# Expert tokens of a mixture-of-experts decoder step: rows fetched by an indirect DMA instead of one-hot matmuls

## The reference, cut to what matters

```
def moe_swiglu(x, g, w_router, w_eg, w_eu, w_ed):
    h = rms_norm(x, g)
    hf = h.reshape(-1, D_MODEL)
    logits = (hf @ w_router).astype(jnp.float32)
    top_v, top_i = lax.top_k(logits, TOP_K)
    gates = jax.nn.softmax(top_v, axis=-1)
    combine = jnp.einsum('tk,tke->te', gates, jax.nn.one_hot(top_i, N_EXPERTS, ...))
    y = jnp.zeros_like(hf)
    for e in range(N_EXPERTS):
        he = jax.nn.silu(hf @ w_eg[e]) * (hf @ w_eu[e])
        y = y + combine[:, e:e + 1] * (he @ w_ed[e])
    return x + y.reshape(x.shape)
```

## Time and profile before

| | |
|---|---|
| median of 3 runs | 1717.1 us (1715.7 to 1719.49) |
| span of the profiled execution | 1712.6 us |
| TensorE matmul busy | 1595.5 us (93%) |
| VectorE busy | 1169.5 us (68%) |
| ScalarE busy | 954.3 us (56%) |
| GpSimd busy | 673.6 us (39%) |
| DMA | 426.00 MB, mean 249 GB/s |
| mean granted TensorE clock | 0.963 |
| share of the chain of waits that ended last | TensorE 75%, VectorE 13% |

### The profile page before, as it was taken

How to read it: one execution, slowest core, us unless ns; L and a number is a source line. 1 busy time by engine, 2 the same in 40 slices (tenths; PEclk the granted TensorE clock), 3 DMA queues, 4 the chain that set the end, 5 groups by cost and what they waited for, 6 DMA issues and landing times.

```text
span 1712.6 us, 22726 instructions
## 1 busy us (share of the span) xinstructions
PE 1595.5 (93%) x8152; PEld 1334.1 (78%) x8152; DVE 1169.5 (68%) x1150; ACT 954.3 (56%) x991; POOL 673.6 (39%) x235
## 2 busy tenths in 40 slices
PE   6786899999978889999999999999999999999998
PEld 5774899999956868878877877877877887887786
DVE  5998545446784447767767776776786776777775
ACT  5411543344553426756756657666666665766664
POOL 5561111012210025545436445444544544553553
PEclk9888999999987879999999999999999999999999
DMA  8821244444450139969978987987996996996993
GB/s 317 153 94 54 74 148 176 154 142 170 144 210 1 50 139 338 352 246 364 355 266 342 356 328 277 351 333 279 346 349 273 355 351 247 359 358 241 366 348 146
DMA packets 62801, 426.00 MB, mean 249 GB/s; under 512 B 7653, under 2 KB 9957, under 8 KB 12192
## 3 DMA queue, kind: packets, MB, share of 16 engines
q1 hardware_dynamic: 57312, 412.38, 64.4%
q0 software_dynamic: 2432, 8.08, 2.5%
q10 hardware_dynamic: 3008, 4.88, 0.9%
HBM read 418.36 MB, written 7.95 MB: 249 GB/s over the span
## 4 chain that ended last, share of the span: by engine, by line
PE 75%; DVE 13%; issue 7%; ACT 4%; POOL 1%; DMA 0%; ACTq 0%; DVEq 0%
PE bank L326 21%; PE bank L328 21%; PE bank L327 20%; PE bank L662 4%; DVE odd L1142 2%; ACT w_hi L995 2%; DVE C L1142 2%; PE bank L686 2%; DVE w_lo L1087 2%; PE bank L703 2%; DVE pick L1414 1%; PE bank L348 1%; PE bank L582 1%; DVE C L1155 1%; DVE w_lo L1363 0%
## 5 line engine op out<-in xcount | busy, mean ns | idle before, releaser
L1580 POOL TENSOR_TENSOR d_lo<-land,d_hi 128x2048 fp32r<-128x2048 f32 x112 | 538.8, 4814 | 664.9 <-ACT d_hi L998 664.9
L1363 DVE TENSOR_TENSOR w_lo<-land,w_hi 128x2048 fp32r<-128x2048 f32 x224 | 611.9, 2767 | 157.9 <-ACT w_hi L995 157.0
L995 ACT CAST w_hi<-land 128x2048 fp32r<-128x2048 f32 x224 | 417.6, 1912 | 0.0
L326 PE MATMUL bank<-w_hi,xe_hi 128*128 128x512 f32 x896 | 376.0, 420 | 0.5 <-DVE w_lo L1363 0.5
L328 PE MATMUL bank<-w_hi,xe_lo 128*128 128x512 f32 x896 | 353.0, 394 | 0.0
L327 PE MATMUL bank<-w_lo,xe_hi 128*128 128x512 f32 x896 | 350.5, 391 | 0.0
L998 ACT CAST d_hi<-land 128x2048 fp32r<-128x2048 f32 x112 | 214.2, 1914 | 128.9 <-PE bank L328 128.9
L326 PEld LDWEIGHTS bank<-w_hi,xe_hi 128*128 128x128 f32 x896 | 168.8, 188 | 39.7 <-DVE w_lo L1363 7.5
L328 PEld LDWEIGHTS bank<-w_hi,xe_lo 128*128 128x128 f32 x896 | 168.5, 188 | 38.0
L327 PEld LDWEIGHTS bank<-w_lo,xe_hi 128*128 128x128 f32 x896 | 169.3, 189 | 33.2
L326 PE MATMUL bank<-d_hi,heT_hi 128*128 128x512 f32 x448 | 176.8, 395 | 19.7 <-DVE heT_lo L1458 19.7
(11 more groups left out here) (227 smaller groups left out, 2355.9 us busy)
## 6 DMA issues: line engine op xcount, KB each, us to landing
land<-in_w_expert SPq DMA_DIRECT2D x336, 1024.0 KB, 6.7
land<-in_w_dense SPq DMA_DIRECT2D x54, 1024.0 KB, 4.8
rel_rows<-rb POOLq DMA_DIRECT2D x1, 3072.0 KB, 38.0
bias<-rel_rows ACTq DMA_DIRECT2D x4, 512.0 KB, 4.8
X<-in_x SPq DMA_DIRECT2D x4, 288.0 KB, 5.8
out_y<-X SPq DMA_DIRECT2D x2, 576.0 KB, 2.8
Us<-in_state POOLq DMA_DIRECT2D x1, 1088.0 KB, 9.4
out_conv_s<-Us POOLq DMA_DIRECT2D x1, 1088.0 KB, 6.7
```

The lines of the kernel that those rows point to most:

```text
L326: pe.matmul(out, w[0], x[0], start=start, stop=False)
L995: act.copy(w_hi[n % RING][:], land[(DENSE + u) % LAND][:]).then_inc(hi_done, 1)
L1363: dve.tensor_tensor(w_lo[n % RING][:], land[slot][:], w_hi[n % RING][:].bitcast(F32), ALU.subtract).then_inc(split, 1)
L1580: pool.tensor_tensor(d_lo[ch % 2][:], land[slot][:], d_hi[ch % 2][:].bitcast(F32), ALU.subtract).then_inc(d_split, 1)
```

## The change

`H_tok` is now scaled by the inverse norm when it is made (half 0 by GpSimd, half 1 by ScalarE) and stored once to a DRAM tensor `h_rows` of 289 rows, the last of them zero. `PG` is gone, and `pick` holds ones only. A small matmul (slot_rows: `pick` x `tok`, 2 columns, three token tiles) gives for each of the expert's 128 slots the row of its token and its gate. VectorE turns the first into an integer `slot_row`, and GpSimd starts an indirect DMA that fetches 128 rows of 4 KB (0.5 MB) from `h_rows` to `xt`, one row to a partition. gather is then eight plain transposes of `xt`. The gate is applied per slot when `oe` is taken from PSUM, and `oe` is kept in two fp32r parts: ScalarE writes both halves of oe_hi, VectorE both halves of oe_lo. back becomes two fp32r matmuls by `PT`, which now holds ones. The split of the down weights stays on GpSimd.

```diff
-            def gather(h):
+            def gather(trip, h):
+                pe.wait_ge(xt_ready, 16 * (trip + 1))
                 for k in range(4):
-                    for j, (t0, nt) in enumerate(TT):
-                        last = pe.matmul(bank[4 + h][:, P * k:P * k + P],
-                                         H_tok[0:nt, j, (4 * h + k) * P:(4 * h + k + 1) * P],
-                                         pick[0:nt, j, :], start=(j == 0), stop=(j == 2))
+                    last = pe.transpose(bank[4 + h][:, P * k:P * k + P], xt[:, (4 * h + k) * P:(4 * h + k + 1) * P], ident)
+            def slot_rows(out):
+                for j, (t0, nt) in enumerate(TT):
+                    last = pe.matmul(out[:, 0:2], pick[0:nt, j, :], tok[0:nt, j, :], start=(j == 0), stop=(j == 2))
+                last.then_inc(rows_placed, 1)
...
+            pe.wait_ge(P_ready, 1)
+            slot_rows(bank[0])
             pe.wait_ge(htok_ready, 6)
...
-                pe.matmul(out[:, 0:T], oe[:, P * k:P * k + P], PT[:, :], start=True, stop=True).then_inc(y_done, 1)
+                pe.matmul(out[:, 0:T], oe_hi[:, P * k:P * k + P], PT[:, :], start=True, stop=False)
+                pe.matmul(out[:, 0:T], oe_lo[:, P * k:P * k + P], PT[:, :], start=False, stop=True).then_inc(y_done, 1)
...
+                    if ch == GATES_AT + 1:
+                        with pe.If(trip < n_trips - 1):
+                            pe.wait_ge(P_ready, trip + 2)
+                            pe.wait_ge(PT_ready, trip + 2)
+                            slot_rows(bank[7])
...
+            act.wait_ge(htok_scaled, 3)
+            act.wait_ge(htok_ready, 6)
+            for i, (t0, nt) in enumerate(TT):
+                act.dma_start(h_rows[t0:t0 + nt, :], H_tok[0:nt, i, :]).then_inc(h_stored, 16)
...
-                act.copy(oe[:, 0:512], bank[2][:, :]).then_inc(oe_ready, 1)
+                act.wait_ge(gates_ready, trip + 1)
+                for h in range(2):
+                    act.activation(oe_hi[:, 512 * h:512 * h + 512], bank[2 + h][:, :], ACT.Identity,
+                                   scale=slot_gate[:, 0:1]).then_inc(oe_hi_ready, 1)
...
+            def slot_row_of(n, src):
+                dve.wait_ge(rows_placed, n)
+                dve.tensor_scalar(slot_row[:], src[:, 0:1], -1.0, float(T), ALU.mult, ALU.add).then_inc(rows_ready, 1)
...
+                    if ch == GATES_AT + 2:
+                        with dve.If(trip < n_trips - 1):
+                            slot_row_of(trip + 2, bank[7])
-                dve.tensor_copy(oe[:, 512:1024], bank[3][:, :]).then_inc(oe_ready, 1)
+                for h in range(2):
+                    dve.wait_ge(oe_hi_ready, trip * 2 + h + 1)
+                    dve.scalar_tensor_tensor(out=oe_lo[:, 512 * h:512 * h + 512], in0=bank[2 + h][:, :],
+                                             scalar=slot_gate[:, 0:1], in1=oe_hi[:, 512 * h:512 * h + 512].bitcast(F32),
+                                             op0=ALU.mult, op1=ALU.subtract).then_inc(oe_ready, 1)
+                with dve.If(trip < n_trips - 1):
+                    dve.wait_ge(oe_ready, trip * 2 + 4)
+                    dve.tensor_copy(slot_gate[:], bank[7][:, 1:2]).then_inc(gates_ready, 1)
...
+            def gather_rows(trip):
+                pool.wait_ge(rows_ready, trip + 1)
+                pool.indirect_dma_start(xt[:], None, h_rows[:, :],
+                                        bass.IndirectOffsetOnAxis(ap=slot_row[:, 0:1], axis=0)).then_inc(xt_ready, 16)
...
+            pool.wait_ge(h_stored, 48)
+            gather_rows(0)
             expert_lo(0, 0)
             expert_lo(0, 1)
...
                 with pool.If(trip < n_trips - 1):
+                    gather_rows(trip + 1)
                     expert_lo(trip, NCH)
                     expert_lo(trip, NCH + 1)
```

More of the change, by code:

```diff
@@ L172, in build @@
                ("d_lo0", [P, UNIT], F32R), ("d_lo1", [P, UNIT], F32R),
-               ("H_tok", [P, 3, D], F32), ("pick", [P, 3, SLOTS], F32), ("PG", [P, 3, SLOTS], F32),
-               ("PT", [SLOTS, T], F32), ("slot_of", [P, 3, PASSES * NE + 1], F32),
+               ("oe_hi", [SLOTS, D], F32R), ("oe_lo", [SLOTS, D], F32R), ("pick", [P, 3, SLOTS], F32),
+               ("PT", [SLOTS, T], F32R), ("tok", [P, 3, 2], F32), ("slot_row", [SLOTS, 1], I32),
+               ("slot_gate", [SLOTS, 1], F32), ("slot_of", [P, 3, PASSES * NE + 1], F32),
                ("gate_of", [P, 3, PASSES * NE + 1], F32), ("lg", [P, 6, 3, NE], F32), ("rt", [P, 3], F32),
                ("cmp", [P, 2, 3, NE, NE], F32), ("top", [P, 16], F32), ("trips", [1, 2], I32)]
[L177 to L182, removed]
+        (d_hi0, d_hi1, d_lo0, d_lo1, oe_hi, oe_lo, pick, PT, tok, slot_row, slot_gate, slot_of, gate_of, lg, rt,
+         cmp_, top, trips, xe_hi, xe_lo, xt, silu_g, he, heT_hi, heT_lo) = phase(
+            *moe, ("xe_hi", [P, D], F32R), ("xe_lo", [P, D], F32R), ("xt", [SLOTS, D], F32),
+            ("silu_g", [P, CH], F32), ("he", [SLOTS, CH], F32), ("heT_hi", [P, CH], F32R), ("heT_lo", [P, CH], F32R))
+        Hm, H_tok, zero_row = phase(*moe, ("Hm", [P, KT_D, T], F32), ("H_tok", [P, 3, D], F32),
+                                    ("zero_row", [1, D], F32))[-3:]
         d_hi, d_lo = [d_hi0, d_hi1], [d_lo0, d_lo1]
@@ L610, in route_sums @@
                 if k == KT_D - 1:
-                    pe.matmul(STAT[:, 0:32], ident, PT[:, 0:32], start=False, stop=True).then_inc(lg_done, 1)
+                    pe.matmul(STAT[:, 0:32], ident, pick[:, 0, 0:32], start=False, stop=True).then_inc(lg_done, 1)
             def to_tokens(k):
@@ L1366, in _ @@
             dve.wait_ge(kv_stored, 80)
-            dve.memset(oe[:], 0.0).then_inc(oe_ready, 2)
-            dve.memset(PT[:], 0.0).then_inc(PT_ready, 1)
+            dve.memset(oe_hi[:].bitcast(F32), 0.0).then_inc(oe_ready, 1)
+            dve.memset(oe_lo[:].bitcast(F32), 0.0).then_inc(oe_ready, 1)
+            dve.memset(pick[:], 0.0).then_inc(pick_zero, 1)
+            dve.memset(PT[:].bitcast(F32), 0.0).then_inc(PT_ready, 1)
+            dve.memset(zero_row[:], 0.0).then_inc(zero_made, 1)
+            seq(dve.tensor_reduce(top[:, 13:14], c("before"), AX.X, ALU.add))
+            for i, (t0, nt) in enumerate(TT):
+                dve.tensor_scalar(tok[:, i, 0:1], top[:, 13:14], float(T - t0 - (P - 1)), None, ALU.add)
             for d in range(KT_D):
@@ L1379, in _ @@
             dve.wait_ge(sd_ready, 5)
-            seq(dve.reciprocal(rt[:], rt[:]))
+            dve.reciprocal(rt[:], rt[:]).then_inc(rt_inverse, 1)
+            dve.wait_ge(rt_inverse, 1)
             dve.wait_ge(lg_done, 1)
```

56 lines of the change are left out of this document (36 added, 20 removed).

## The result

The changed kernel takes 1743.1 us in the median of 4 runs (1742.3 to 1744.2), the kernel before 1717.4 beside it: a ratio of 1.0151, with a 95% interval of 1.0140 to 1.0163. It is slower by 25.8 us. The forecast was slower by 8.5 (1725.6 us, range 1708 to 1746). The span is 1740.5 us, against 1712.6: 27.9 us more. (The sum of the forecast is one of spans; the device time of the changed kernel lies 2.6 us above its span, and not 4.5 as the forecast carried it.)

A forecast was written before the change was run, and what follows sets the result against it. Bound taken: TensorE and w_lo/d_lo taking turns on one port, equally long at 8.96 us a chunk. Seams 17.5, eighth trip -0.3, tail +1.1, ahead of trip 0 -9.8: +8.5, 1725.6 us, range 1708 to 1746.

The forecast's parts named there:

- the sign and the mechanism of the seam: Slower, chance 0.63; at each seam TensorE waits for a fetch issued behind the w_lo pair of chunk 12: +2.6 us.
- L: At each seam, TensorE's wait from row numbers to landed rows: 5.7 us, the middle of 4.8 and 6.7.
- the formula: Whole-span change: 7 x (L - 3.2) - 9.0 us; L = 2.2 gives 1701, L = 9.4 gives 1751.5.
- the fetch waits its turn behind the weights (L near 8): Rival at the seams: fetch queued behind weight landings, +16 us, 1742; with a low clock up to 1753; chance 0.18.
- The Trainium skill's fit: For a GpSimd DMA alone, 2.0 us + bytes / 436 GB/s: 3.2 us for the fetch, whole sum near 1708.
- the term ahead of trip 0: Before the first trip: picks run at once, gate_up starts at 611.7 instead of 621.43, -9.8 us (bounds -5 and -13).
- the trip's end: Both oe_lo halves and the gate's copy ahead of he(0): turn(0) 0.9 us later, but only 0.2 stays.
- the clock at nothing: At each seam TensorE idles about 8 us and the clock falls; cost nothing, or up to 1.6 a trip without cover.
- The row numbers: At each seam: slot_row ready at 749.2, behind the pair of w_lo of chunk 12 that formerly ended at 749.26.
- The chunks: Per trip: scatter -0.3 us, place -0.5; slot_rows about 0.7 on TensorE, otherwise hidden.
- the saved 13.4 us of TensorE: Fp32r scatter saves 0.21 us, 64 times; w_lo and d_lo taking turns at 8.96 leave only 2.4 of it.
- Tail and eighth trip: After the last trip oe_hi and oe_lo in series, +1.1 us; the eighth trip's back, -0.3.

The follow-up runs named there:

- experiment 5: The changed kernel with 256 of the 1024 channels stored and fetched as rows, a quarter of the fetch's bytes (work left out): 1737.1 us.
- experiment 9: The changed kernel with only a quarter of the columns of each expert's weight units 5, 6 and 7 landing (work left out): 1728.7 us.
- Experiment 7: The changed kernel with VectorE's xe_rest moved ahead of the last pair of w_lo before trip 0: 1740.7 us.
- Experiment 12: The changed kernel with fetch ahead of d_lo(13), row numbers behind he(12), xe_rest ahead of the w_lo before trip 0, a seam's second w_lo behind heT_lo(13): 1681.1 us.
- experiment 11: The changed kernel with xt and an unused tile ahead of xe_hi, giving xe, silu_g, he and heT their addresses in the kernel before: 1740.7 us.
- experiment 4: The changed kernel with GpSimd splitting only half of each down unit in the loop, the other half of d_lo keeping old data: 1723.0 us.
- experiment 13: The kernel of Experiment 12 with the two oe_lo and the gate's copy moved behind he(0) of the next trip: 1662.8 us.
- experiment 10: The changed kernel with an unused tile of 32 bytes a partition ahead of xe_hi, so xe, xt, he and heT begin on multiples of 64 bytes: 1747.4 us.
- experiment 1: The changed kernel with slot_row written ahead of the pair of w_lo instead of behind it, the fetch still behind d_lo(13): 1732.5 us.

## Why the prediction was right or wrong

**Right: the sign and the mechanism of the seam.** The 8.5 us of gather matmuls at a seam are gone and the seam is longer. The fetch is issued right behind the pair of w_lo, and the transposes end their wait with the DMA into `xt`. What follows cuts each trip at the row numbers, the first transpose, down(13) and turn(0); all are means of seven.

**Wrong: the size of L, the time from row numbers to rows.** This is the step that failed. I took 5.7 us; the seam above has 8.06, and the mean of seven is 7.6. By the formula this is 7 x 1.9 = 13 us, two thirds of the miss of 19.4 between the spans. Two things were off. First, a hand-over of 0.8 us from `slot_row` to the issue (883.01 to 883.82), which I had left out when I compared L with rows that count from the issue. Second, 1.0 us in the landing (6.7 in the mean for 5.7), by the choice between the rows. I took the middle of a 512 KB transfer (4.8) and a weight unit in the stream (6.7), though I had said that the queues would be full. The load was what counted: 6.8 in full queues, as the weight unit, 4.5 in thin ones and 4.3 in quiet ones (experiments 5 and 9). The row to take was the one under the same load. My rival "the fetch waits its turn behind the weights (L near 8)" had this mechanism and a chance of 0.18, and what I held against it, that a queue of its own should get its share, was the argument that failed. That its 1742 us is within 1.2 of the measured time is partly luck: with the measured L of 7.6 the formula gives 1739, and the terms below make up the rest. The Trainium skill's fit, quoted in the prediction ("DMA: Bandwidth & Descriptors", section "Anatomy of one DMA — SWDGE (gpsimd) path"), gives an estimated 3.2 us for the landing; 4.3 was measured in quiet queues and 6.8 in full ones.

**Wrong in the term ahead of trip 0.** -9.8 forecast, -5.4 measured. The rows came when expected (606.07 against 607 to 608), but I let the w_lo ahead of xe_lo wait for one d_lo, and it waited for both, 11.17 us. The earlier trace rows had shown it: there three small picks waited 8.64 us for both. Experiment 7 took the wait away and turn(0) came 6.3 us earlier.

**Wrong: the trip's end.** +0.2 forecast, +0.73 measured (13.20 from down(13) to turn(0) where the clock adds nothing, against 12.47 in the earlier trace rows). With the two halves of oe_lo VectorE needs 1.9 us from its last w_lo to he(0), where it needed 0.5. I had this hidden by the wait of the next w_lo, but the two chunks behind turn(0) got no shorter (17.8 us, before 17.7). Seven times 0.5 is 4 us.

**Nearly right: the clock at nothing.** It falls to 0.50 (1.2 GHz) at each seam. In four of seven that costs nothing: turn(0) is held by the chain of VectorE up to he(0), and the clock is back before. In the other three turn(0) comes 0.1, 0.6 and 0.7 us later, 1.4 us in all, since the clock stays low for 4.5, 5.4 and 5.8 us after down(13) starts. In the last of them he(0) is done at 1471.01, and TensorE comes to it 0.8 us later:

```profile
1470.59 0.42 DVE L1492 TENSOR_TENSOR he<-silu_g,bank 128x256 f32<-128x256 f32 x1 [0.34 <-issue]
1471.83 0.38 PE L718 MATMUL bank<-con,he 128*128 128x128 f32 x2
```

Experiment 12 shows the clock's price where the cover is gone.

**The row numbers came sooner than forecast.** From turn(0) to the end of the pair of w_lo, or now of `slot_row`, it was 118.1 us and is 117.1: -1.05, where -0.35 was forecast (-0.3 of the scatter and -0.05 in the sum of times). The pair took 4.89 us in the new seam and not 5.80, because slot_rows holds turn(12) back but not d_lo(13), which therefore ends sooner after it. Seven times 0.7 is 5 us, against the other misses.

**The chunks: right in total, with luck in the parts.** From turn(0) to turn(12) the forecast has -0.3 for the scatter, -0.5 for place and +0.7 for slot_rows, together -0.1; -0.2 was measured. Place gave 1.07 of idle time back (2.62 to 1.55) and slot_rows took 0.81; and TensorE's slower pace took away what its bare chunks would have gained: turn(10) to turn(11) rose from 9.08 to 9.20. That the saved 13.4 us of TensorE would not come through held (8.96 to 8.90 in a chunk), but in the changed kernel mostly for a reason that the forecast did not have: of the 0.21 us saved in a chunk the slower pace took back up to 0.15. The reason that it did have, w_lo and d_lo at one port, shows by itself in experiment 11, at the old pace: 8.86 us with a back and 8.84 without, where TensorE alone would need some 8.73 (8.88 of experiment 4 less 0.15).

**Misread: the earlier trace rows.** I took the start of the d_lo at 829.07 as caused by the end of the pair. The row itself says that ScalarE's d_hi ended the wait; it ended at 828.99, and the end of the pair at 829.10 was a coincidence of the chain in experiment 11. The pair does wait for the d_lo; the d_lo does not wait for the pair. And the cycle is 8.86 and not the 8.96 at which I had it level with TensorE.

**Tail and eighth trip.** +0.8 forecast, +1.3 measured.

In sum: +8.5, plus 13.2 for L, 1.2 for the stretch from the first transpose to down(13) (2.93 us for 2.75), 3.7 at the trip's end, 1.4 for the clock, 4.4 ahead of trip 0 and 0.5 for the tail, less 4.9 for the earlier row numbers, gives 28.0; the difference of the spans is 27.9.

## What to carry to other kernels

A transfer's price under load is read from a row under the same load, not from one of the same size: here the weight stream in the queues made 4.3 us into 6.8, and a quarter of the bytes saved only 0.7. When a fetch takes the place of arithmetic, issue it a whole step before it is used: the change lost 1.5% with its row numbers and its issue behind a pair of w_lo and a d_lo, with these moved it was 1.5% faster than before, and with three more moves of order (experiments 7, 12 and 13) 3.2%. Before a wait is removed, look at what is level with it (here the one-hot, he(13), he(0) and the clock, one after another), and where two engines exclude each other as VectorE and GpSimd do here, a small instruction can wait for all that the other has in its queue (8.64 us for a pick, 11.17 for a w_lo). Two events that fall together in every chunk need not be cause and effect; look at what the row says ended the wait.

## What the runs showed of the hardware that was not expected

- Where small tiles stand in SBUF changes the pace of three-pass fp32r matmuls of 512 columns: every 0.2291 us with `xe_hi` 52160 bytes of a partition behind the start of the d_hi tiles and `heT_hi` 62400, every 0.2332 with `xe_hi` at 46624 and `heT_hi` at 60960, and 0.2336 with both 32 bytes further (offsets by the tiles' order and sizes in the kernels). The moving tiles stood at the same addresses in all. `xe`, `he` and `heT` are the stationary tiles, but `silu_g` and `xt` moved with them, so that it is the stationary tile is likely and not shown. What about the addresses decides is open: a multiple of 64 bytes is not it (experiment 10).
- The issue of an indirect DMA on GpSimd took 2.86 us instead of 0.96 while VectorE ran the pair of w_lo (experiment 1).
- Transfers of 128 rows of 1 KB take 3.1 us alone and 6.1 in full queues, of 4 KB 4.3 and 6.8 (experiment 5 and the profile after), and 4.5 with three thin landings around them (experiment 9).
- An idle time of 2.39 us on TensorE was enough for the granted clock to fall to 0.50 in five of seven seams (experiment 12); with waits of up to 0.7 us it stayed at 1.00 there (experiment 13).
